# A second copy of the sample state in block order, and the transposes of C moved from TensorE to VectorE

## The reference, cut to what matters

```
num = (jnp.einsum('btsh,bshd->bthd', s, vb)
       + sc_inter[..., None] * jnp.einsum('bhvk,bthk->bthv', C, qb))
den = jnp.sum(s, axis=2) + sc_inter * jnp.einsum('bhk,bthk->bth', n, qb)
h = num / jnp.maximum(jnp.abs(den), jnp.exp(-m_row))[..., None]
...
C_new = decay[..., None, None] * C + jnp.einsum('bsh,bshv,bshk->bhvk', ws, vb, kb)
...
merged = sigmoid(ga) * (yA @ w_pa) + sigmoid(gb) * (yB @ w_pb); out = merged @ w_out
```

## Time and profile before

| | before |
|---|---|
| median of 3 runs | 1523.41 us (1523.41 to 1523.42) |
| the profiled execution | 1523.64 us, of which the span is 1522.1 us |
| granted TensorE clock | 0.997 of full speed, mean |
| PE busy | 1504.9 us, 99% |
| PEld busy | 1498.3 us, 98% |
| DVE busy | 892.8 us, 59% |
| ACT busy | 658.2 us, 43% |
| POOL busy | 174.9 us, 11% |
| DMA | 268.06 MB, mean 176 GB/s |

### The profile page before, as it was taken

One profiled execution on the slowest core, in us unless ns is written; L12 is line 12 of the kernel. 1 busy time (PEld: TensorE's weight loads), 2 busy tenths in 40 slices (PEclk: granted clock), 3 DMA queues, 4 the chain that ended last, 5 costly groups with the idle time before them and its releaser, 6 DMA issues.

```text
span 1522.1 us, 31157 instructions
## 1 busy us (share of the span) xinstructions
PE 1504.9 (99%) x11379; PEld 1498.3 (98%) x11379; DVE 892.8 (59%) x1542; ACT 658.2 (43%) x932; POOL 174.9 (11%) x315
## 2 busy tenths in 40 slices
PE   9999999999999999999999999999999999999996
PEld 9999999999999999999999999999999999999996
DVE  7755555654444457766767676666766644444444
ACT  6433433333333345454545454545454433333442
POOL 4000000001000003121121303031312000000000
PEclk9999999999999999999999999999999999999998
DMA  7765555556555555564747484847474655555543
GB/s 231 207 167 150 168 160 166 147 175 221 166 164 165 165 166 142 177 204 152 229 123 258 115 267 113 269 115 257 125 252 130 196 152 177 154 173 185 169 155 136
DMA packets 238658, 268.06 MB, mean 176 GB/s; under 512 B 12728, under 2 KB 227456, under 8 KB 237760
## 3 DMA queue, kind: packets, MB, share of 16 engines
q1 hardware_dynamic: 221360, 226.26, 49.5%
q0 software_dynamic: 17008, 41.25, 7.9%
q10 hardware_dynamic: 256, 0.10, 0.0%
HBM read 244.48 MB, written 23.06 MB: 176 GB/s over the span
## 4 chain that ended last, share of the span: by engine, by line
PE 93%; issue 5%; DVE 1%; DMA 0%; ACT 0%; POOL 0%; DVEq 0%; POOLq 0%; ACTq 0%
PE ps L396 27%; PE ps L397 27%; PE ps L398 27%; PE ps L572 2%; PE ps L560 2%; PE ps L584 1%; PE ps L691 1%; PE ps L624 1%; PE ps L529 1%; DVE otok L1509 0%; DMA xt<-in_x_prompt_dram 0%; PE ps L656 0%; PE ps L405 0%; ACT hb L760 0%; PE ps L430 0%
## 5 line engine op out<-in xcount | busy, mean ns | idle before, releaser
L998 DVE TENSOR_TENSOR wlo<-raw,whi 128x1024 fp32r<-128x1024 f32 x416 | 508.0, 1224 | 547.3 <-ACT whi L743 545.6
L396 PE MATMUL ps<-xh,whi 128*128 128x288 f32 x2560 | 764.8, 299 | 0.0
L743 ACT ACTIVATE whi<-raw 128x1024 fp32r<-128x1024 f32 x416 | 440.3, 1059 | 739.9 <-PE ps L398 719.4
L398 PE MATMUL ps<-xh,wlo 128*128 128x288 f32 x2560 | 755.3, 295 | 0.0
L397 PE MATMUL ps<-xl,whi 128*128 128x288 f32 x2560 | 754.5, 295 | 0.0
L396 PEld LDWEIGHTS ps<-xh,whi 128*128 128x128 f32 x2560 | 481.0, 188 | 0.3
L397 PEld LDWEIGHTS ps<-xl,whi 128*128 128x128 f32 x2560 | 480.8, 188 | 0.2
L398 PEld LDWEIGHTS ps<-xh,wlo 128*128 128x128 f32 x2560 | 480.6, 188 | 0.0
L397 PE MATMUL ps<-yl,whi 128*128 128x288 f32 x512 | 151.5, 296 | 0.0
L396 PE MATMUL ps<-yh,whi 128*128 128x288 f32 x512 | 150.8, 294 | 0.0
L398 PE MATMUL ps<-yh,wlo 128*128 128x288 f32 x512 | 150.6, 294 | 0.0
(11 more groups left out here) (325 smaller groups left out, 1280.8 us busy)
## 6 DMA issues: line engine op xcount, KB each, us to landing
raw<-in_w_in_dram SPq DMA_DIRECT2D x320, 512.0 KB, 3.7
raw<-in_w_pb_dram SPq DMA_DIRECT2D x32, 512.0 KB, 3.5
Cin<-in_state_mlstm_C_dram POOLq DMA_DIRECT2D x16, 1024.0 KB, 8.8
out_dram<-Cin POOLq DMA_DIRECT2D x16, 1024.0 KB, 6.3
raw<-in_w_pa_dram SPq DMA_DIRECT2D x32, 512.0 KB, 3.5
raw<-in_w_out_dram SPq DMA_DIRECT2D x32, 512.0 KB, 3.6
out_dram<-cpo POOLq DMA_DIRECT2D x8, 256.0 KB, 2.4
xres<-in_x_prompt_dram SPq DMA_DIRECT2D x1, 2048.0 KB, 8.4
```

The lines of the kernel that those rows point to most:

```text
L396: nc.tensor.matmul(out, whi[:, c, kk, cols], mh_[:, k, :], start=(k == 0), stop=False)
L398: last = nc.tensor.matmul(out, wlo[:, c, kk, cols], mh_[:, k, :], start=False, stop=(k == KT - 1))
L743: nc.scalar.activation(whi[:, c], raw[:, c], ACT.Copy).then_inc(hi_ready, 1)
L998: nc.vector.tensor_tensor(wlo[:, c], raw[:, c], whi[:, c].bitcast(F32), ALU.subtract).then_inc(lo_ready, 1)
```

## The change

C is loaded twice. Beside `Cin`, which stays for the update, POOL loads `Xb` in block order: partition group g of 32 holds, for value index s in a block of 32, the keys 64g to 64g + 63 of every value block. DVE turns it by 32x32 blocks into `Yb` (`turn_blocks`), which puts keys on the partitions. ACT and DVE split that as before, now from SBUF; `CTl` lies over `Yb`, with two buffers. The keys are in another order on the partitions than before, so q and n are brought into that order by eight small operations on 32 partitions each (`KEY_BLOCKS`). `part` shrinks to one product, and POOL stores each to DRAM and loads it back in the last stage. The wait for `Cin` moves from PE to DVE.

```diff
+KEY_BLOCKS = [(rows_of(n // 2), rows_of(n % 4), n % 2, n // 4) for n in range(8)]
...
-    part = a("part", [P, KT, T])
+    Xb = a("Xb", [P, NB, 8, 2, 32])
+    part = a("part", [P, 2, T])
+    part_d = nc.dram_tensor("part_d", (8, P, 2 * T), F32)
...
+    CTl = nc.alloc_sbuf_tensor_at("CTl", [P, 2, 2, DH], F32R, offset=a.at)
+    Yb = a("Yb", [P, 2, 2, DH])
     CTh = a("CTh", [P, 2, DH + 2], F32R)
-    CTl = a("CTl", [P, 2, DH + 2], F32R)
...
@@ PE @@
-        def c_turn(h, b):
-            if b % 4 == 0:
-                pe.wait_ge(c_in[b // 4], 16 * h + 16)
-            if b >= 2:
-                pe.wait_ge(ct_lo, 8 * h + b - 1)
-            for kh in range(2):
-                for vh in range(2):
-                    last = pe.transpose(ps[:, X6 + b % 2, DH * kh + P * vh:DH * kh + P * vh + P],
-                                        Cin[:, b, vh, P * kh:P * kh + P], ident[:])
-            last.then_inc(ct_t, 1)
...
+                nc.tensor.matmul(ps[:, X4, 0:DH + 2], qm[:, kh, 2 * S * b:2 * S * b + P], CTh[:, kh, :],
+                                 start=(b == 0 and kh == 0), stop=False, skip_group_check=True)
+                last = nc.tensor.matmul(ps[:, X4, 0:DH], qm[:, kh, 2 * S * b:2 * S * b + P],
+                                        CTl[:, b % 2, kh], start=False,
+                                        stop=(b == NB - 1 and kh == 1), skip_group_check=True)
...
-                c_turn(h, c)
...
-                c_turn(h, 4 + c)
...
-                    nc.tensor.matmul(ps[:, X4, 0:DH + 1], W[:, 384:512], vtok_h[:, 2, :],
+                    nc.tensor.matmul(ps[:, X4, 0:DH + 2], W[:, 384:512], vtok_h[:, 2, :],
...
@@ ACT @@
+            act.wait_ge(yg_lo, GROUPS)
             nc.scalar.activation(tg[:], results(0), ACT.Tanh, scale=0.5).then_inc(slot_free[0], 1)
...
         def ct_copy(h, b):
-            act.wait_ge(ct_t, 8 * h + b + 1)
-            nc.scalar.activation(key_major(CTh), turned(b), ACT.Copy).then_inc(ct_ev, 1)
+            act.wait_ge(block_turned, 8 * h + b + 1)
+            if b > 0:
+                act.wait_ge(inter_mm, 8 * h + b)
+            nc.scalar.activation(CTh[:, :, 0:DH], of_c(b), ACT.Copy).then_inc(ct_ev, 1)
...
@@ DVE @@
-            step(nc.vector.tensor_copy(nTh[:], n_turned))
+            for out_, in_, kt_out, kt_in in KEY_BLOCKS:
+                last = nc.vector.tensor_copy(nT[out_, kt_out, :, 1].bitcast(F32), n_turned[in_, kt_in, :])
+            step(last)
+            step(nc.vector.tensor_copy(nT[:, :, :, 0], nT[:, :, :, 1].bitcast(F32)))
...
+            dve.wait_ge(part_free, i + 1)
+            nc.vector.scalar_tensor_tensor(part[:], tg[:], 1.0, ps[:, 2:4, 0:T], ALU.add,
                                            ALU.mult).then_inc(slot_free[1], 1)
...
-            for t, n in ((CTh, nTh), (CTl, nTl)):
-                nc.vector.tensor_copy(t[:, :, DH:DH + 1], n[:, :, ds(h + 8 * b, 1)].bitcast(F32))
-            nc.vector.tensor_tensor(key_major(CTl), turned(b), key_major(CTh).bitcast(F32),
+            nc.vector.tensor_copy(CTh[:, :, DH:DH + 2], nT[:, :, ds(h + 8 * b, 1), :].squeeze(2).bitcast(F32))
+            nc.vector.tensor_tensor(CTl[:, b % 2], of_c(b), CTh[:, :, 0:DH].bitcast(F32),
                                     ALU.subtract).then_inc(ct_lo, 1)
+
+        def turn_blocks(h, b):
+
+            if b % 4 == 0:
+                dve.wait_ge(block_in[b // 4], BLOCK_LOADS * 16 * (h + 1))
+            if b >= 2:
+                dve.wait_ge(inter_mm, 8 * h + b - 1)
+            nc.vector.transpose(of_c(b).rearrange("p k (j s) -> p j k s", s=32),
+                                Xb[:, b]).then_inc(block_turned, 1)
...
         def add_state(h, b):
+            if b % 4 == 0:
+                dve.wait_ge(c_in[b // 4], 16 * h + 16)
...
-                    qs(nc.vector.tensor_tensor(scb[:], qk[:, 0:2, TP:T], scb[:], ALU.mult))
-                    scaled = scb[:].rearrange("p k (b t) -> p k b t", t=TS)
+                    for out_, in_, kt_out, kt_in in KEY_BLOCKS:
+                        last = nc.vector.tensor_tensor(qp[out_, kt_out, :], qk[in_, kt_in, TP:T], scb[in_, kt_in, :],
+                                                       ALU.mult)
+                    qs(last)
+                    scaled = qp[:].rearrange("p k (b t) -> p k b t", t=TS)
...
                     last.then_inc(qm_set, 1)
+                    turn_blocks(h, 0)
...
                 ct_split(h, c)
+                turn_blocks(h, c + 1)
...
                 ct_split(h, 4 + c)
+                if c < 3:
+                    turn_blocks(h, 5 + c)
...
+            dve.wait_ge(part_in, 16 * i + 16)
+            nc.vector.tensor_tensor(sm[:], tm[:], part[:], ALU.add).then_inc(ma_sum, 1)
...
@@ POOL @@
+        def load_blocks(h, half_):
+            for b in range(4 * half_, 4 * half_ + 4):
+                for g in range(4):
+                    pool.dma_start(Xb[rows_of(g), b].rearrange("s j k r -> s j (k r)"),
+                                   C_blocks[:, b, ds(h, 1), :, 64 * g:64 * g + 64].squeeze(1)
+                                   ).then_inc(block_in[half_], 16)
...
         load_hist(0)
+        load_blocks(0, 0)
+        load_blocks(0, 1)
+        with pool.Fori(0, 8) as i:
+            pool.wait_ge(slot_free[1], MB_USE[1] + 1 + i)
+            pool.nop(nofuse=True)
+            pool.dma_start(part_d[ds(i, 1)].squeeze(0), part[:].rearrange("p j t -> p (j t)")).then_inc(part_out, 16)
+            pool.wait_ge(part_out, 16 * i + 16)
+            pool.sem_inc(part_free, 1)
...
                 load_hist(h + 1)
+                pool.wait_ge(block_turned, 8 * h + 4)
+                pool.nop(nofuse=True)
+                load_blocks(h + 1, 0)
             pool.wait_ge(var_set, h + 1)
...
             if more:
+                pool.wait_ge(block_turned, 8 * h + 8)
+                pool.nop(nofuse=True)
+                load_blocks(h + 1, 1)
 
                 pool.wait_ge(cst_out, 256 * h + 256)
...
+        load_part(0)
+        with pool.Fori(1, 8) as i:
+            pool.wait_ge(ma_sum, i)
+            pool.nop(nofuse=True)
+            load_part(i)
```

More of the change, by code:

```diff
@@ L55, with rows_of @@
 NEW_BANK = (2, 3, 5)
+BLOCK_LOADS = 16
+def rows_of(g):
+    return slice(32 * g, 32 * g + 32)
+KEY_BLOCKS = [(rows_of(n // 2), rows_of(n % 4), n % 2, n // 4) for n in range(8)]
 EPS = 1e-6
@@ L127, in build @@
     nacc = fixed("nacc", [P, 2, NB + 1, HEADS])
-    nTh = fixed("nTh", [P, 2, NB * HEADS], F32R)
-    nTl = fixed("nTl", [P, 2, NB * HEADS], F32R)
+    nT = fixed("nT", [P, 2, NB * HEADS, 2], F32R)
     half = fixed("half", [P, 3])
@@ L206, in build @@
     scb = a("scb", [P, 2, S])
+    qp = a("qp", [P, 2, S])
     qk = a("qk", [P, 4, T])
@@ L326, in x_bank, with of_c @@
         return 2 + k % 6
[L329 to L333, removed]
+    def of_c(b):
+        return Yb[:, b % 2]
     @block.sync
@@ L665, in _ @@
                     pe.wait_ge(vt_ev, h + 1)
-                    nc.tensor.matmul(ps[:, X6, 0:DH + 1], W[:, 0:P], vtok_h[:, 0, :], start=True, stop=True)
-                    nc.tensor.matmul(ps[:, X7, 0:DH + 1], W[:, P:TP], vtok_h[:, 0, :], start=True, stop=False)
-                    nc.tensor.matmul(ps[:, X7, 0:DH + 1], W[:, TP:TP + P], vtok_h[:, 1, :], start=False,
+                    nc.tensor.matmul(ps[:, X6, 0:DH + 1], W[:, 0:P], vtok_h[:, 0, 0:DH + 1], start=True, stop=True)
+                    nc.tensor.matmul(ps[:, X7, 0:DH + 1], W[:, P:TP], vtok_h[:, 0, 0:DH + 1], start=True, stop=False)
+                    nc.tensor.matmul(ps[:, X7, 0:DH + 1], W[:, TP:TP + P], vtok_h[:, 1, 0:DH + 1], start=False,
                                      stop=True)
-                    nc.tensor.matmul(ps[:, X4, 0:DH + 1], W[:, 384:512], vtok_h[:, 2, :],
+                    nc.tensor.matmul(ps[:, X4, 0:DH + 2], W[:, 384:512], vtok_h[:, 2, :],
                                      start=False, stop=True, skip_group_check=True).then_inc(num_mm, 1)
@@ L1414, in _ @@
                     dve.wait_ge(num_mm, h + 1)
-                    for t, (n, bank) in enumerate(((P, 6), (P, 7), (S, 4))):
-                        last = nc.vector.tensor_copy(f3[0:n, t:t + 1], ps[0:n, bank, DH:DH + 1])
+                    for t in range(2):
+                        nc.vector.tensor_copy(f3[:, t:t + 1], ps[:, 6 + t, DH:DH + 1])
+                    last = nc.vector.tensor_reduce(f3[0:S, 2:3], ps[0:S, 4, DH:DH + 2], mybir.AxisListType.X, ALU.add)
                     den = Steps(dve, den_step, 3 * h)
@@ L1466, in _ @@
             dve.wait_ge(slot_free[1], MA_USE[1] + i + 1)
-            nc.vector.tensor_tensor(sm[:], tm[:], part[:, ds(2 * i, 2), :], ALU.add).then_inc(ma_sum, 1)
+            dve.wait_ge(part_in, 16 * i + 16)
+            nc.vector.tensor_tensor(sm[:], tm[:], part[:], ALU.add).then_inc(ma_sum, 1)
             dve.wait_ge(ma_hi, i + 1)
@@ L1644, in _, with load_part @@
         h_body(HEADS - 1, more=False)
+        def load_part(i):
```

(3 more changed lines are left out.)

13 lines of the change are left out of this document (8 added, 5 removed).

## The result

The changed kernel is slower: 1579.07 us (1578.1 to 1581.99, four runs) against 1523.41, a ratio of 1.0368 with a 95% interval of 1.0355 to 1.0381. Forecast were 1510.7 us and faster. The profiled execution took 1579.79 us, its span 1578.3.

A forecast was written before the change was run, and what follows sets the result against it. PE was taken to bound the kernel (93% of the span). Per head, 3.52 us of removed transposes less the stalls gave 1.6; eight heads 12.8, with columns 12.9, so 1523.64 became 1510.7 us, range 1503 to 1518.

The forecast's parts named there:

- DMA: Loads per head: 2 MB more add 0.08 to 0.32 to a share of 0.60, 0.92 at worst; weights stay in time.
- Rival D: Weight loads: small pieces make weights late, ACT's `whi` waits, then everything; at 2 us per head 1527; chance 3%.
- Transposes: PE, C work: each `c_turn` of four transposes costs 0.44 us; removing all 64 saves 28.2 us.
- Ledger, term by term: PE stalls per head: 0.10, 0.55, 0.70 at b=0, 1, 2, 0.48 before the q-k product, 0.10 before V transposes.
- Products: DVE: eight 32-lane q products replacing one take 0.8 us instead of 0.25, 0.6 more; bounds 0.4 to 1.2.
- Turn: DVE block turn of C, 128x512: 0.74 us long, occupying 0.65 back to back; length bounds 0.31 to 1.24.
- rival B: DVE's turn is dear, occupying 1.0 us or more; gain gone near 0.99, 1529.5 us at 1.15; chance 8%.
- POOL: POOL's queue: 0.66 us per block-load issue, bounds 0.62 and 1.39; 16 ahead of `rstd` stay hidden, 3.6 us to spare.
- Rival C: POOL late: issues over 0.88 us make `rstd` late in 7 of 8 heads; at 1.1 us 1534.5; chance 7%.
- `part` through DRAM, n columns, c_in: DRAM parking of a product, n-column copies (about 1.5 us of DVE once) and later reload of C: all costed at nothing.
- Rival A: All hidden: the turns fit into DVE's idle third of a head; 1495 to 1500 us; chance 8%.

The follow-up runs named there:

- e2: Changed kernel without the second half of the block loads (sequences 4 to 7, between store and reload of C) after the first head; 1511.52 us.
- e7: Changed kernel with the second half of the block loads moved behind `rstd` and the reload of C held until the next head's q is scaled; 1511.16 us.
- e1: Changed kernel without either half of the block loads after the first head, so later heads turn stale blocks; 1510.92 us.
- e13: Changed kernel with second block loads behind `rstd`, reload of C late, `kv4` before turn 4, C work ahead of weight chunks on DVE and ACT; 1498.51 us.
- e14: e13 with turns 0 and 1 moved ahead into the k pair; 1498.57 us.
- e5: Changed kernel with block loads still 64 KB to 32 partitions, but in pieces of 1 KB, fetching wrong blocks; 1549.36 us.
- e10: Changed kernel with block loads still 64 KB in 256-byte pieces, but each spread over 128 partitions, fetching wrong blocks; 1553.49 us.
- e9: Changed kernel with each half of the block loads as one 1 MB DMA over 128 partitions in 2 KB pieces, wrong row order; 1545.14 us.

## Why the prediction was wrong

The step that failed is the one headed DMA: "2 MB more per head. The head moves 187 GB/s at a share of 0.60 ... 0.92 at worst, under 1. A weight chunk lands most of a pair before its use." It spread the new megabytes over 80 us. They stand in two places, and one of them was already at a share of 1.03 to 1.05 (the windows of before, above), with the weights at the very rate at which PE uses them. There was no room, and a mean share of 0.92 can't say so. The cushion was misjudged too: landings of 6.6 us in the median had grown to 15.2, more than the 12.8 us of a pair. Taking the second half out there (e2: 1511.52) or moving it and the reload (e7: 1511.16) brings the time back to the forecast, and nothing else that was tried does so without touching DVE's order.

The change also moved the reload. It stands behind 16 issues now, and both halves go out together at 646.33. Before, POOL let them out one by one, as the store landed:

```profile
641.72 0.75 POOL L1592 DMA_DIRECT2D Cin<-in_state_mlstm_C_dram  x1 [3.86 <-DMA out_dram<-Cin]
645.49 0.76 POOL L1592 DMA_DIRECT2D Cin<-in_state_mlstm_C_dram  x1 [3.02 <-DMA out_dram<-Cin]
```

The prediction had only looked at who reads `Cin` next, not at what the reload would meet.

The loss in PE's own terms: e1 and the changed kernel have the same PE instructions. Idle time is 25.2 us (1509.4 less 1484.2) against 82.8, 57.6 more; busy time is 1484.2 against 1495.5, 11.3 more, which is put down to the slow clock after each long wait. Over the seven heads that have a reload before them that is 8.2 and 1.6 us each, and together the 68.9 us between their spans. Rival D named this mechanism, late weights, with 3% and 2 us a head; its size was 9.8.

The other steps:

- *Transposes.* PE's line is gone, and e1's span is 12.7 us under before, of 28.2 that the transposes took by the prediction's estimate: stalls of 15.5 against 15.4 (8 x 1.93) forecast. Only 8.0 of them are idle time (25.2 less 17.2); the rest are delays so short that the length of the matmul before covers them. Right in sum.
- *Ledger, term by term.* In e1 `inter(0)` starts at 662.88 where it was due at 662.26, one matmul spacing after 662.13: 0.62 late, 0.46 of it idle (0.10 forecast). The next two are 4.02 and 4.22 apart where PE's pace is 3.66, so 0.36 and 0.56 (0.55 and 0.70), and the product 3.92 after, 0.26 (0.48). In sum 1.80 against 1.83: the first is mis-sized by the products, 0.52 too small, and the others are 0.55 too large together. That the sum fits so well, and with it that e1 comes within 0.2 us of 1510.7, is in part luck.
- *Products.* Eight take 1.55 us, 182 ns each and no overlap; 0.8 was taken. That is 1.3 more than the single product of before, where 0.6 was forecast and 1.2 was the upper bound, so it lies a little over the bound.
- *Turn.* 704 ns against 740; the next instruction starts 0.62 after it (669.52 to 670.14), against 0.65. Right; rival B is out.
- *POOL.* An issue takes 586 ns, against 660, with turns on DVE beside it. `rstd` is never late: POOL waits for DVE there in all 8 heads. Rival C is out, and no issue is longer than 709 ns. The margin in the second head, for which 3.6 us were forecast, is 3.4 here and 2.4 in e7; it is least in the first head, 1.6.
- *`part` through DRAM, n columns, c_in.* e1 holds them all and comes out at the forecast; no wait for `part` is among those of DVE. Costed at nothing, rightly as far as 0.2 us can tell.
- *Rival A.* Its 1495 to 1500 needed the transfers moved and another order of the queues: e13 and e14 reach it.

## What to carry to other kernels

A DMA share is read over the stretch in which the new transfers will stand, not over the loop body: there, compare the rate of the queue that feeds the bottleneck with the rate at which it eats. Count what else is issued in that stretch, and what the new issues push into it. And where engines work in order, everything behind a late chunk is late with it, so put short urgent work ahead of it, and bulk transfers where the DMA engines have room.

## What the runs showed of the hardware that had not been expected

- At a full share, 64 KB loads to 32 partitions in 256-byte pieces, mixed with the weights, move 202 to 232 GB/s from 644 to 652 us, where large transfers move 373 to 377. With either of the two traits alone it is 263 (e5) and 283 (e10) from 648 to 652. In time they don't add: about 4 and 8 us alone over e9, 34 together.
- POOL's queue took 79.7% of the DMA engines' time from 637 to 646 us, while weight loads were waiting in the other; in the kernel before it had 72.8% of the same stretch.
- In an idle stretch of 9 us the clock granted to PE falls to 0.50, and PE then works 4.6 us at it (672.05 to 676.68). The 15 projection matmuls in it are 0.24 us apart, which loses 1.6 us; the busy time of the whole kernel is 11.3 us over that of e1, 1.6 for each of the seven long waits.
- Eight small products on 32 partitions, six of them from one group of partitions to another, start 0.195 us apart, while small copies on the same engine start 0.08 apart. Whether the kind of operation or the groups make the difference was not tried.
